# Mixed tiles handed over in SBUF with their squares summed on VectorE, and the scan's drive products on two row tiles

## What is computed

```
h = rmsnorm(x, g_mix);  z = h @ w_in            # q | k | v | u | gate_a | gate_s
bu_re = einsum('gpc,btgc->btgp', bb_re, u)      # the drive of the scan: 64 groups, 16 channels -> 64 states
bu_im = einsum('gpc,btgc->btgp', bb_im, u)
h_re, h_im = associative_scan(...)              # complex diagonal state space
y = C_re h_re - C_im h_im + d_skip * u
x = x + (gate_a * branch_a + gate_s * branch_s) @ w_out
x = x + peer_ffn(rmsnorm(x, g_ffn), ...)        # rmsnorm: x * rsqrt(mean(x*x) + eps) * g
x = x + (p @ w_ple) * sigmoid(rmsnorm(x, g_ple) @ w_ple_gate)
```

## Time and profile before

| what | value |
| --- | --- |
| median of 3 runs | 4517.93 us (4517.27 to 4521.38) |
| the profiled execution, its own time | 4516.09 us |
| its span in the profile | 4514.3 us |
| mean granted PE clock | 0.977 |
| scan stage, barrier to barrier | about 166 to 667 us |
| mix ends, out begins | about 1543 to 1547 us |
| out ends, route and hidden begins | about 1757 to 1758 us |

### The profile page before, as it was taken

One profiled execution on the slowest core, in us unless ns is written; L12 is line 12 of the kernel. 1 busy time (PEld: TensorE's weight loads), 2 busy tenths in 40 slices (PEclk: granted clock), 3 DMA queues, 4 the chain that ended last, 5 costly groups with the idle time before them and its releaser, 6 DMA issues. The chain is left out here.

```text
span 4514.3 us, 79902 instructions
## 1 busy us (share of the span) xinstructions
PE 4271.5 (95%) x29732; PEld 4070.4 (90%) x29732; DVE 2658.2 (59%) x4340; ACT 1532.0 (34%) x2466; POOL 2615.9 (58%) x2018
## 2 busy tenths in 40 slices
PE   7899997999998898999899999999799999999999
PEld 6788887888787897999899999999799999999899
DVE  4477765664334302678566666654478888777721
ACT  3122213444443323223233333333333333333332
POOL 5678762222222342445566667757689888777543
PEclk9999998999999999999999999999999999999999
DMA  4233333334984542333499999879899999898533
GB/s 115 68 95 93 94 84 93 114 103 157 374 307 140 192 115 76 98 94 125 150 328 329 337 331 345 319 284 324 315 381 393 396 396 396 348 386 344 230 100 95
DMA packets 366838, 1023.06 MB, mean 227 GB/s; under 512 B 45826, under 2 KB 119298, under 8 KB 303778
## 3 DMA queue, kind: packets, MB, share of 16 engines
q1 hardware_dynamic: 264274, 552.12, 36.7%
q0 software_dynamic: 52192, 370.71, 21.6%
q10 hardware_dynamic: 50160, 97.41, 5.7%
HBM read 936.41 MB, written 83.62 MB: 226 GB/s over the span
## 5 line engine op out<-in xcount | busy, mean ns | idle before, releaser
L252 PE MATMUL rt_acc<-xn_act,rt_w_hi 128*128 128x384 f32 x4096 | 1063.6, 340 | 34.1 <-POOL rt_w_rest L242 33.7
L2812 PE MATMUL val_y_ps<-val_wt,val_v 128*128 128x352 f32 x6144 | 999.0, 324 | 35.5 <-DVE val_wt L2887 28.6
L242 POOL TENSOR_TENSOR rt_w_rest<-rt_w_raw,rt_w_hi 128x512 fp32r<-128x512 f32 x576 | 735.8, 1302 | 508.4 <-ACT rt_w_hi L237 506.1
L2812 PEld LDWEIGHTS val_y_ps<-val_wt,val_v 128*128 128x128 f32 x6144 | 988.2, 190 | 45.6 <-issue 41.9
L252 PEld LDWEIGHTS rt_acc<-xn_act,rt_w_hi 128*128 128x128 f32 x4096 | 740.3, 188 | 49.0 <-POOL rt_w_rest L242 45.5
L2755 POOL TENSOR_TENSOR val_v<-val_v_raw,val_v 128x1024 fp32r<-128x1024 f32 x256 | 613.9, 2411 | 148.8 <-ACT val_v L2843 146.7
L252 PE MATMUL rt_acc<-xn_act,rt_w_rest 128*128 128x384 f32 x2048 | 692.8, 338 | 0.0
L2656 DVE CUSTOM_DVE_ANT_0 rt_space<-rt_space,rt_mid 128x2048 f32<-128x2048 f32 x160 | 361.3, 2282 | 245.8 <-DMA rt_space<-in_peer_u,out_row_id 239.7
L2899 DVE SCALAR_TENSOR_TENSOR val_row_ps<-val_rows,val_row_w,val_row_ps 128x2048 f32<-128x2048 f32 x189 | 444.3, 2351 | 0.1
L237 ACT ACTIVATE rt_w_hi<-rt_w_raw 128x512 fp32r<-128x512 f32 x576 | 335.4, 626 | 287.2 <-PE rt_acc L252 190.5
L2922 DVE TENSOR_TENSOR out_xT<-out_xT,val_y_ps 128x352 f32<-128x352 f32 x512 | 265.3, 518 | 228.0 <-PE val_y_ps L2812 227.9
(11 more groups left out here) (444 smaller groups left out, 7386.0 us busy)
## 6 DMA issues: line engine op xcount, KB each, us to landing
rt_w_raw<-in_peer_uT SPq DMA_DIRECT2D x512, 256.0 KB, 5.8
val_v_raw<-in_peer_vp SPq DMA_DIRECT2D x128, 1024.0 KB, 9.4
scan_w_raw<-in_w_in SPq DMA_DIRECT2D x128, 256.0 KB, 3.1
att_w_raw<-in_w_in SPq DMA_DIRECT2D x96, 256.0 KB, 3.3
hid_scratch<-rt_hid ACTq DMA_DIRECT2D x128, 192.0 KB, 4.3
val_hid<-hid_scratch SPq DMA_DIRECT2D x32, 768.0 KB, 7.9
gate_scratch<-rt_space ACTq DMA_DIRECT2D x11, 2048.0 KB, 10.8
val_gate<-gate_scratch SPq DMA_DIRECT2D x32, 704.0 KB, 11.9
```

Of the source, the lines that this page charges most:

```text
L242: e.tensor_tensor(self.rest[:, s, 0:nk, :], self.raw[:, r, 0:nk, :], self.hi[:, s, 0:nk, :].bitcast(F32), ALU.subtract).then_inc(self.rest ...
L252: mm = e.matmul(acc[:, h, 0:width], w[:, s, k, :], act[:, kt0 + k, a, col + h * width:col + (h + 1) * width], start=first and k == 0 and w ...
L2812: mm = e.matmul(y_ps[:, t % 2, 0:VTOK], v[:, c % 2, a, j, t * P:(t + 1) * P], wt[:, g % 2, j, b, :], start=j == 0 and a == 0 and b == 0, s ...
```

## The change

- **Drives on two row tiles.** Copies of the imaginary table and of u are made on other partitions: `B_next` and `u_next` hold them rotated by 32 partitions (`turned_rows`). The real matmul of a drive reads partitions a, the imaginary one partitions b, which are 32 before them around the circle. The copies are DMAs from SBUF to SBUF: ACT issues four of them ahead of `D`, SP two ahead of the first weights. PE waits for them before the first drive (`B_in`, `u_in`).
- **Scan loops written out** on ACT and SP.
- **Mixed tiles stay in SBUF.** `k.xT` (16 tiles of x) now lies at the bottom of SBUF for the whole program; the scan's tables, the first page buffer and `qk_sample` lie in it until the mix. `stage_mix` writes its tiles there, `stage_out` splits them from there, and x is then loaded over them, two tiles at a time, once they are split (`rest_ready`).
- **Squares summed in `stage_out`.** ACT squares each finished x tile between two weight units, DVE adds the squares up in `sums` (`add_squares`), and PE sums over the partitions at the end of the stage (`column_sums`, the last tile by itself). ACT loads the table of the square root one tile before the end (`early_root`). `Norm` keeps the root, the reciprocal and the split of the tiles; its loop is written out with four `scaled` buffers and DVE's rest and scale by turns, and ACT splits a weight unit behind each four tiles instead of four units ahead of all.
- Order of loads: `w_out` comes first in `stage_out`, the query weights first in `stage_route_hidden`.

```diff
+def column_sums(e, total, part, ones, first, last):
+    for h in range(2):
+        mm = e.matmul(total[:, h, 0:HALF], ones, part[:, h * HALF:(h + 1) * HALF], start=first, stop=last)
+    return mm
...
 class Norm:
+    def scalar(self, e, tiles):
+        for t in tiles:
+            if t == 0:
+                e.activation(halves(self.deviation[:]), self.total[:, :, 0:HALF], ACT.Sqrt, scale=1.0 / D_MODEL,
+                             bias=self.c("eps")).then_inc(self.dev_ready, 1)
+            e.wait_ge(self.scaled_ready, t + 1)
+            e.activation(self.out[:, t, 0, :], self.scaled[:, t % 4, :], ACT.Copy).then_inc(self.hi_ready, 1)
...
+        scale(0)
+        scale(1)
+        for t in range(KT):
+            rest(t)
+            if t + 2 < KT:
+                scale(t + 2)
...
 stage_scan:
+        turned_rows = ((slice(0, 96), slice(32, P)), (slice(96, P), slice(0, 32)))
         @block.sync
-            with e.Fori(0, N1) as i:
+            for out, rows in turned_rows:
+                e.dma_start(u_next[out, 0, :], k.uT[rows, 0, 0:NP]).then_inc(u_in[0], 16)
+            for i in range(N1):
                 for u in range(PER1):
         @block.scalar
+            for out, rows in turned_rows:
+                e.dma_start(B_next[out], k.BT[rows, 1]).then_inc(B_in, 16)
+            for out, rows in turned_rows:
+                e.dma_start(u_next[out, 1:CT, :], k.uT[rows, 1:CT, 0:NP]).then_inc(u_in[1], 16)
             for t in range(CT):
                 e.activation(k.D[:, t, :], k.c("ident"), ACT.Copy, scale=k.ssm_d_col[:, t:t + 1]).then_inc(d_staged, 1)
...
-            body1(0, first=True)
-            with e.Fori(1, N1 - 1) as i:
-                body1(i)
-            body1(N1 - 1, last=True)
+            for i in range(N1):
+                body1(i, first=i == 0, last=i == N1 - 1)
...
             def drive(i, q):
                 e.wait_ge(bu_free, i * 4 + (q + 1))
-                t, r = i + q // 4, slice(32 * (q % 4), 32 * (q % 4) + 32)
-                for c in range(2):
-                    mm = e.matmul(bu[q % 2][:, c, :], k.BT[r, c, t, :], k.uT[r, t, 0:NP], start=True, stop=True)
-                mm.then_inc(bu_ready, 1)
+                t, a, b = i + q // 4, 32 * (q % 4), 32 * ((q + 3) % 4)
+                if q % 4 == 0 and t < 2:
+                    e.wait_ge(u_in[t], 32)
+                e.matmul(bu[q % 2][:, 0, :], k.BT[a:a + 32, 0, t, :], k.uT[a:a + 32, t, 0:NP], start=True, stop=True)
+                e.matmul(bu[q % 2][:, 1, :], B_next[b:b + 32, t, :], u_next[b:b + 32, t, :], start=True,
+                         stop=True).then_inc(bu_ready, 1)
...
 stage_mix:
-            store(KT - 1)
-            for a in range(2):
-                e.wait_ge(mix_stored[a], 16 * (KT // 2))
-                e.tensor_tensor(mix[:, c % 2, :], a_part[:], x, ALU.add).then_inc(mix_ready, 1)
+                e.tensor_tensor(k.xT[:, c, :], a_part[:], x, ALU.add).then_inc(mix_ready, 1)
...
 stage_out:
         @block.sync
+            for c in range(KT):
+                for u in range(U):
+                    w.load(e, 0, 0, c * U + u, columns(k.w_out, c, UNIT * u))
+                if c % 2:
+                    e.wait_ge(rest_ready, c + 1)
+                    e.dma_start(k.xT[:, c - 1:c + 1, :], k.x_dram[:, c - 1:c + 1, :]).then_inc(x_in[c // 2], 16)
...
         @block.scalar
+            for v in range(U):
+                for t in range(v * UNIT, (v + 1) * UNIT):
+                    e.activation(k.act[:, t, 0, :], k.xT[:, t, :], ACT.Copy).then_inc(hi_ready, 1)
+                w.split_hi(e, 0, 0, v)
+            for u in range(RING, KT * U):
+                w.split_hi(e, 0, 0, u)
+                if u >= 2 * U and u % U == 0:
+                    square(u // U - 2)
+            square(KT - 2)
+            e.activation(early_root[:], k.c("eps"), ACT.Sqrt)
+            square(KT - 1)
         @block.tensor
+            e.wait_ge(summed, KT - 2)
+            column_sums(e, k.end, sums[:], k.c("ones"), True, False)
+            e.wait_ge(sq_ready, KT)
+            column_sums(e, k.end, sq[:, (KT - 1) % 2, :], k.c("ones"), False, True).then_inc(total_ready, 1)
+            e.wait_ge(total_ready, 1)
         @block.vector
+            for c in range(KT):
+                e.wait_ge(x_in[c // 2], 16)
+                if c >= 2:
+                    add_squares(c - 1)
+                w.wait_used(e, 0, 0, (c + 1) * U)
+                x = halves(k.xT[:, c, :])
+                e.tensor_tensor(x, x, acc[c % 2][:, :, 0:HALF], ALU.add).then_inc(added, 1)
```

More of the change, by code:

```diff
@@ L316, in load @@
[L316 to L350, removed]
+    def __init__(self, s, x, gain, out, const, total, work):
+        self.x, self.gain, self.out, self.c, self.total = x, gain, out, const, total
+        self.deviation, self.rstd, self.scaled = work
+        self.dev_ready, self.rstd_ready = s.sem("dev_ready"), s.sem("rstd_ready")
+        self.scaled_ready, self.hi_ready, self.rest_ready = s.sem("scaled_ready"), s.sem("n_hi_ready"), s.sem("n_rest_ready")
@@ L2031, in _ @@
                     open_gate(gates.index((part, c)))
-                if part == ATT and c:
-                    store(c - 1)
-            store(KT - 1)
-            for a in range(2):
-                e.wait_ge(mix_stored[a], 16 * (KT // 2))
         @block.vector
@@ L2149, in _ @@
             w.credit_used(e)
-            def body(i, first):
-                for a in range(2):
-                    e.wait_ge(acc_free, i * 2 + (a + 1))
-                    for u in range(U):
-                        if first and a == 0:
-                            e.wait_ge(rest_ready, (u + 1) * UNIT)
-                        w.multiply(e, i, PER, a * U + u, acc[a], k.act, u * UNIT, u == 0, u == U - 1)
-            body(0, True)
-            with e.Fori(1, KT // 2) as i:
-                body(i, False)
+            for c in range(KT):
+                e.wait_ge(added, c + 1)
+                for u in range(U):
+                    if c == 0:
+                        e.wait_ge(rest_ready, (u + 1) * UNIT)
+                    w.multiply(e, 0, 0, c * U + u, acc[c % 2], k.act, u * UNIT, u == 0, u == U - 1)
@@ L2298, in _ @@
         def _(e):
-            e.dma_start(keysT[:], k.keys_T).then_inc(keys_in, 16)
-            norm.load(e)
             for i in range(T_A):
@@ L2367, in queries @@
                 for u in range(PER_A):
-                    if u == 0 and first:
-                        norm.squares(e)
+                    if first and u < U:
+                        norm.scalar(e, range(u * UNIT, (u + 1) * UNIT))
                     w.split_hi(e, 0, 0, i * PER_A + u)
-                    if u == 3 and first:
-                        norm.split(e)
                     if u == 1 and not first:
```

141 lines of the change are left out of this document (54 added, 87 removed).

## The result

The changed kernel takes **4477.35 us** (median of 4 runs, 4473.86 to 4481.69) against 4517.6 for the kernel before (4 runs, 4516.15 to 4521.38): ratio 0.9911, 95% interval 0.9896 to 0.9927. The forecast was 4476, range 4464 to 4498.

The account below looks back on a forecast made before the run. PE bounds out's later groups and the scan's trips; other engines' chains bound the hand-over and norm. Scan 20.6, hand-over 10.1 and norm 11.1 sum to 41.8 us: 4517.9 - 41.8 = 4476 us, range 4464 to 4498.

Parts of the forecast that it names:

- The drive: Scan: two row tiles side by side should cut a drive from 1.91 to 1.06 us, 0.85 us less.
- The rival that it gives nothing: Scan: tiles run in turn, or POOL and DVE hold the step at 14.95 us; total 4497, chance 0.17.
- Who holds the scan back: Scan: PE waits for ACT to empty `acc`, which waits for DVE's divide; two steps take 28.20 to 29.30 us, median 28.73.
- my 17.6: Scan's six looped trips: a trip of 57.19 us saves 2.93, six save 17.6 us (10.7 to 22.3).
- the free rhythm: Rival in the scan: the chain behind the divides does not bind, trips take 56.4 us; total 4471, chance 0.15.
- Table loads: Scan: of twelve ACT table loads of 1.28 us the change keeps one, so the q = 1 step comes earlier.
- Start of the scan: Scan's first groups: first drives wait for copies, yet 2 us gained (bounds 2 lost, 3.5 gained).
- Hand-over: From mix's end through out's first group: no store to wait for, weights loaded first; 10.1 us gained (8 to 11.5).
- rests end at 1554.4, 1557.8 and 1561.2: Out's first group: times its further rests are done, so PE works until 1562.5 and with unit 3 until 1565.6.
- 9.2 us behind the last mixed add instead of 15.1: Sign to look for at out's start: when PE's first product of out comes, 9.2 us instead of 15.1.
- Norm: Behind out: squares hidden in out, 1.45 us per tile from the first scale; 11.1 us gained (8.5 to 13).
- PE's clock, the rival for a slower kernel: Scan: new short PE waits bring the granted clock down to 1.2 GHz; whole scan at that clock 4870, chance 0.02.

Follow-up runs that it names:

- the third profile of this scan: Changed kernel with the squares of tiles 0 to 14 taken only behind out's last add: 4490.42 us, 12.1 over the changed kernel.
- the last experiment: Changed kernel with five edits: evacuation ahead of store, y stores set apart, copies later, POOL held in out, earlier query weight splits in norm: 4465.21 us, ratio 0.9884 to before.
- the evacuation first: Changed kernel, but in the scan ACT empties `acc` before the store that waits for the divide: 4470.07 us, 8.2 under the changed kernel.
- the second execution: The changed kernel run once more with nothing edited: 4478.29 us (5 runs, 4472.9 to 4480.57).
- the second execution of the scan's part alone: Kernel before with only the scan's changes (two row tiles, copies, written-out loops), run again: 4502.32 us, 18.2 under the kernel before.

## Why the prediction was right, and where its terms were off

- **The drive** (0.85 us a step): right, and shown by taking the row tiles away. The rival that it gives nothing is out.
- **Who holds the scan back:** the mechanism was right (the chain behind the divide, and q = 1 as the late step), but in the two profiles of the changed kernel it binds in two of six trips, not in all (the third profile of this scan has four late steps). Two inputs failed. I took the divides' lengths over from the old rhythm, median 1.25; a divide waits out the POOL operation that it meets, and in the new rhythm it mostly meets the end of one, median 0.82. That the phase decides, the rule of the Trainium skill weighed there (SBUF — State Buffer, section SBUF: two separate sides), was the better guide. And the q = 1 step was not 25.75 us in every trip: it is 25.8 where ACT issues its four y stores in 1.9 us, but 26.8 where they take 3.1, which delays a weight split and so POOL, and 26.9 where the one table load stands ahead of them. That the y stores are the cause fits the last experiment, which sets them apart: 25.8 in every trip. The last group of the scan, which has no drive ahead of it, shows the chain once more: it comes 14.01 behind the one before, and 13.08 with the evacuation first. The trips gained 19.35, between my 17.6 and the free rhythm's 22.3.
- **Table loads:** that the written-out loop makes q = 1 early enough is shown by the loop put back. I had spoken of the loads as a side effect; the loop is worth 11 us. The load takes 1.28 us with the Gelu 0.02 us behind it (load from 419.46, Gelu at 420.76 in that kernel). The Trainium skill's page ScalarE: Activation LUTs (section What ACT_TABLE_LOAD costs) adds a drain of 1.38 us to each switch; no such gap stands in these rows.
- **Start of the scan** (2 us gained): 0.8. ACT's first weight split came 2.3 us later (172.84 against 170.58), as taken; the first PE group came 2.8 later, and the interval to the second, with the drive at the lower clock, shrank by 1.2, not 1.85. With fewer copies ahead of the first weights the fifth group comes 2.1 us sooner (241.05). But this stretch repeats poorly: seven executions with this start of the scan have the fifth group at 242.7 to 245.1, the two with the old one at 242.2 and 244.0. So neither a gain at the start nor how much the copies cost is shown; that the copies cost something fits the 241.05, which lies below all of them.
- **Hand-over** (10.1): 8.4. The steps up to PE's first product held within 0.1 us. The step that failed is "rests end at 1554.4, 1557.8 and 1561.2": I priced DVE's rests at their undisturbed length beside POOL's splits. The last rest ended 20.4 us behind mix's last add, not 17.7 as the working has it. Holding POOL back gave 2.2 us. No experiment parts the two changes ahead of PE's start, no store to wait for and `w_out` loaded first: that both count is the prediction's working, which held. The closing sentence of the prediction, "9.2 us behind the last mixed add instead of 15.1", names the wrong start: these are the intervals from mix's last matmul (9.14 and 15.18 measured); from the add the working has 7.5.
- **Norm** (11.1): 9.5. The squares are hidden as said and are what carries it. The step that failed is the same one: 1.45 us a tile, where the trace has 1.33 undisturbed and 1.0 more for each of three collisions; and the first scale was 0.4 later.
- The rule on the shared port (the Trainium skill, SBUF — State Buffer, section SBUF: two separate sides) agrees with all of this: 0.71 becomes up to 1.82 for a rest, 0.78 becomes 1.78 for a scale, both with two SBUF inputs, and only beside a POOL operation. I had used it for the divides alone. PE's clock, the rival for a slower kernel, stayed at 1.00 in the trips. It was 0.50 in one unit behind a long wait of the hand-over in the second execution, 1.5 us of cost; the prediction had named such a case as a bound (8 instead of 10.1).
- The three errors in the scan's start, the hand-over and the norm (4.5 us too much) and those in the trips and later stages (4.9 too little) cancel. That the sum came within 1.4 us of the median is partly luck, all the more as single stages of one program differ by 1 to 3 us between its executions.

## What to carry to other kernels

Price an operation by who runs beside it, not by its median: a change of rhythm here moved the DVE operations with two SBUF inputs against POOL's, and a hold on POOL at the right place gave 2.2 us back and cost nothing in the groups behind. On an in-order queue, put the instruction that another engine waits for ahead of the one that itself waits. And before a step is shortened, look for what only hides behind it: here a loop with its table loads cost at most 2 us at 14.95 us a step, 11 us at 14.10. And read a stage from more than one execution before a gain of 1 to 3 us is put down to an edit.

## What the hardware showed that I had not expected

- The collision works both ways: beside a rest of 1.81 us POOL's split takes 1.77 instead of 1.28 us (pairs at 1535.48 to 1538.68 in the changed kernel): three rests of 1.80 to 1.81 us follow each other beside them, and the next rest takes 0.71 again, when POOL has no unit to split.
- The same four y stores take 1.8 to 3.9 us to issue from ACT's queue within one stage (the second execution of the scan's part alone; 1.8 to 3.1 in the changed kernel), though nothing in the program differs between the trips. Why is open.
- Behind a wait of 1.4 us PE ran on at a granted clock of 1.00, behind one of 3.4 us in the same place at 0.50, for at least the 5.6 us of the unit: a wait of 2.0 us more cost 3.5.
